# Output weights' last row tiles as units of seven products, semaphores awaited at their first users, and extra products at the layer seam

## The reference

```python
u = rmsnorm_2(h, pre_w)
proj = jnp.einsum('btd,de->bte', u, w_in)
...
pool_out = jax.nn.silu(pool_g) * pool_mixer(pool_v, pool_w, pool_scale)
ssd_out = ssd_mixer(ssd_xbc, ssd_z, ssd_dt, conv_w, conv_b, dt_bias, a_log, d_skip, ssd_norm_w)
attn = dsa_attention(q, k, v, qi, ki, i_w, topk).reshape(b, t, ATTN_WIDTH)
attn_out = jax.nn.silu(a_g) * attn
mix = jnp.concatenate([pool_out, ssd_out, attn_out], axis=-1)
out = jnp.einsum('bte,ed->btd', mix, w_out)
return h + rmsnorm_2(out, post_w)
```

## Time and profile before

| | us |
|---|---|
| median of three timed runs | 3298.12 |
| lowest, highest | 3296.45, 3301.9 |
| the profiled execution's own time | 3301.22 |
| its span, first to last instruction | 3299.4 |
| mean granted clock of PE, share of full | 0.994 |
| busy: PE, DVE, ACT, POOL | 3255.6, 1748.0, 770.1, 45.2 |

### The profile page before, as it was taken

One profiled execution on the slowest core, in us unless ns is written; L12 is line 12 of the kernel. 1 busy time (PEld: TensorE's weight loads), 2 busy tenths in 40 slices (PEclk: granted clock), 3 DMA queues, 4 the chain that ended last, 5 costly groups with the idle time before them and its releaser, 6 DMA issues.

```text
span 3299.4 us, 61922 instructions
## 1 busy us (share of the span) xinstructions
PE 3255.6 (99%) x26286; PEld 3003.9 (91%) x26286; DVE 1748.0 (53%) x3298; ACT 770.1 (23%) x2100; POOL 45.2 (1%) x83
## 2 busy tenths in 40 slices
PE   9999999999999999999999999999999999999999
PEld 7998899988999998988999997899879999988898
DVE  2545665414668651513455756666345566566652
ACT  1212322111111201211111226422131122353221
POOL 1000000000000000000000000000000000000000
PEclk9999999999999999999999999999999999999999
DMA  6453345453444304454444444433344545524432
GB/s 223 145 180 111 103 129 158 150 179 117 133 154 128 104 3 144 152 187 115 153 154 153 154 156 126 128 112 120 126 137 148 179 144 163 169 88 128 151 105 102
DMA packets 436210, 454.74 MB, mean 138 GB/s; under 512 B 25051, under 2 KB 412576, under 8 KB 435648
## 3 DMA queue, kind: packets, MB, share of 16 engines
q1 hardware_dynamic: 433344, 443.69, 42.5%
q0 software_dynamic: 2128, 5.19, 0.5%
q10 hardware_dynamic: 464, 1.90, 0.2%
HBM read 448.67 MB, written 2.10 MB: 137 GB/s over the span
## 4 chain that ended last, share of the span: by engine, by line
PE 95%; DVE 2%; ACT 1%; DVEq 1%; issue 0%; ACTq 0%; POOL 0%; POOLq 0%
PE bank L391 43%; PE bank L540 10%; PE bank L2340 9%; PE bank L319 5%; PE bank L2558 3%; PE bank L1965 3%; PE bank L1455 3%; PE bank L2450 1%; PE bank L2465 1%; PE bank L2486 1%; PE bank L2481 1%; PE bank L2475 1%; PE bank L2457 1%; PE bank L2469 1%; PE bank L2424 1%; PE bank L2544 1%
## 5 line engine op out<-in xcount | busy, mean ns | idle before, releaser
L391 PE MATMUL bank<-xnT,ring 128*128 128x128 f32 (+1 forms) x4800 | 593.0, 280 | 2.2 <-ACT wk L1115 1.0
L391 PEld LDWEIGHTS bank<-xnT,ring 128*128 128x128 f32 x4800 | 575.9, 191 | 5.7 <-issue 4.4
L540 PE MATMUL bank<-xnT,ring 128*128 128x256 f32 x1536 | 344.4, 383 | 0.4 <-ACT G L447 0.4
L391 PE MATMUL bank<-hT,ring 128*128 128x128 f32 (+1 forms) x2816 | 338.9, 279 | 0.6 <-ACT G L422 0.5
L391 PEld LDWEIGHTS bank<-hT,ring 128*128 128x128 f32 x2816 | 330.2, 191 | 1.2 <-ACT G L422 1.2
L540 PEld LDWEIGHTS bank<-xnT,ring 128*128 128x128 f32 x1536 | 290.6, 191 | 40.9 <-ACT G L447 0.6
L2340 PE MATMUL bank<-xnT,ring 128*128 128x272 f32 (+1 forms) x1344 | 310.9, 390 | 0.0
L2340 PEld LDWEIGHTS bank<-xnT,ring 128*128 128x128 f32 x1344 | 252.5, 190 | 44.5
L391 PE MATMUL bank<-G,ring 128*128 128x128 f32 (+1 forms) x2128 | 266.3, 278 | 0.0
L391 PEld LDWEIGHTS bank<-G,ring 128*128 128x128 f32 x2128 | 255.0, 191 | 0.2
L459 DVE TENSOR_TENSOR ring<-ring 128x1024 f32<-128x1024 f32 x100 | 122.5, 1225 | 236.6 <-PE bank L391 193.5
(11 more groups left out here) (632 smaller groups left out, 4304.8 us busy)
## 6 DMA issues: line engine op xcount, KB each, us to landing
ring<-in_w_in SPq DMA_DIRECT2D x155, 2048.0 KB, 8.3
ring<-in_w_out SPq DMA_DIRECT2D x16, 3072.0 KB, 11.8
ring<-in_w_out SPq DMA_DIRECT2D x16, 2048.0 KB, 10.6
ring<-in_w_br SPq DMA_DIRECT2D x12, 2048.0 KB, 8.3
ring<-in_w_in SPq DMA_DIRECT2D x6, 512.0 KB, 7.8
G<-in_x POOLq DMA_DIRECT2D x2, 1024.0 KB, 9.2
wk<-in_pool_w POOLq DMA_DIRECT2D x2, 1024.0 KB, 10.6
out<-G SPq DMA_DIRECT2D x8, 256.0 KB, 2.2
```

The lines of the kernel that those rows point to most:

```text
L391: mm = pe.matmul(out_, weights[:, k, :], x(k), start=(start and k == 0), stop=(k == half - 1), skip_group_check=True)
L540: mm = pe.matmul(bank[j][:, META:T], ring[:, s, k, j * P:(j + 1) * P], xnT[:, k, META:T], start=(k == 0), stop=(k == KT - 1))
```

## The change

The tail keeps its first two tiles plain and makes the other 14 by seven short units, as the merges do. Two tiles of each unit are added to `xnT` together, and the squares come in pairs; the first unit's turned inputs and sums are made under the plain tiles.

Several semaphores are awaited later, at the instruction that first needs them: the attention's end (`b2_pe`) at the eighth product of the tail, the merge's end (`merge_done`) at the thirteenth product of the block's end, `st_turned` inside the first unit, the zeroed part of `tok3` in ACT instead of PE. DVE scales inputs in the raw section when half of the second tile is done (`raw_half`), since that half has read the first eight. The gate and low-rank pieces go to bank 1, so that the next unit's bank 0 is free. The sums of the attention's fourth unit move ahead of the first head's scores in DVE's order, and ACT takes more copies ahead of the first head's exponentials. At the seam PE runs 12 products of a matrix of ones, whose result nobody reads.

```diff
@@ raw_section_pe / raw_tiles_dve
                     mm = pe.matmul(bank[j][:, 0:T], ring[:, s, k, j * P:(j + 1) * P], xnT[:, k, :],
                                    start=(k == 0), stop=(k == KT - 1))
+                    if t == 1 and k == KT // 2 - 1:
+                        mm.then_inc(S["raw_half"], 1)
...
-            v.wait_ge(proj_full, t0 + 2)
+            v.wait_ge(S["raw_half"], count["dve"]["raw_half"].go())
             for k in range(8):
                 normalise(k)
+            v.wait_ge(proj_full, t0 + 2)
             out(1).then_inc(proj_free, 1)
@@ mlstm_gates_pe, mlstm_act (rwkv_low_rank_pe, rwkv_act in the same way)
-            pe.wait_ge(proj_free, tiles["pe"].go(2) - 1)
+            pe.wait_ge(proj_free, tiles["pe"].go(2))
             for k in range(KT):
-                mm = pe.matmul(bank[0][0:36, 0:T], ring[:, 0, k, 0:36], xnT[:, k, :], start=(k == 0), stop=(k == KT - 1))
+                mm = pe.matmul(bank[1][0:36, 0:T], ring[:, 0, k, 0:36], xnT[:, k, :], start=(k == 0), stop=(k == KT - 1))
...
+            act.nop().then_inc(proj_free, 1)
             act.wait_ge(proj_full, tiles["act"].go(2))
...
-            act.activation(ROWS[:, FG, :], bank[0][32:36, 0:T], ACT.Copy).then_inc(proj_free, 2)
+            act.activation(ROWS[:, FG, :], bank[1][32:36, 0:T], ACT.Copy).then_inc(proj_free, 1)
@@ block_end_pe (and the wait ahead of its call)
+                    if t == k == 0:
+                        pe.wait_ge(S["part_used"], 3 * (BR - 1) - 1)
+                    if t == 0 and k == 12:
+                        pe.wait_ge(S["merge_done"], 3)
                     pe.matmul(bank[j][:, META:T], ring[:, s, k, j * P:(j + 1) * P], merged[:, k, META:T],
...
-            pe.wait_ge(S["merge_done"], 3)
@@ first units of a stretch (four places)
-                wait("st_turned")
-                    unit_pe(pe, unit_slot(u), unit_from(u, m0), x12, x22, x21, x11, unit_skip(u))
+                    unit_pe(pe, unit_slot(u), unit_from(u, m0), x12, x22, x21, x11, unit_skip(u),
+                            turned=None if u else count["pe"]["st_turned"].go())
@@ layers_pe, layer seam (SEAM = 12)
                     pe.wait_ge(proj_free, tiles["pe"].now(2))
+                    pe.wait_ge(work_free, work["pe"].now(1))
+                    for _ in range(SEAM):
+                        pe.matmul(wbank(work["pe"].now(1))[:, 0:P], ones, ones, start=True, stop=True)
                     raw_section_pe(pe, step)
@@ layers_pe, tail
-                wait("b2_pe")
                 pe.wait_ge(proj_free, tiles["pe"].now(2))
                 pe.wait_ge(S["so_act"], 6 * OUTS * (layer + 1))
-                for s in range(SLOTS):
-                    loaded(s)
-                    for j in range(4):
-                        ...
-                    if s == 2 and layer != LAST:
+                loaded(0)
+                for j in range(2):
+                    pe.wait_ge(proj_free, tiles["pe"].go())
+                    for k in range(W8):
+                        if j == 0 and k == W8 - 1:
+                            wait("b2_pe")
+                        mm = pe.matmul(bank[j][:, m0:T], wide[:, 0, k, j * P:(j + 1) * P], mix[SUB + k][:, m0:T],
+                                       start=(k == 0), stop=(k == W8 - 1))
+                    mm.then_inc(proj_full, 1)
+                for u in range(1, OUTS):
+                    unit_pe(pe, u // 2, m0, *tail_turned, skip=(1 if u == OUTS - 1 else 0), short=tail, part=u % 2,
+                            turned=count["pe"]["st_turned"].go() if u == 1 else None)
+                    if u == 5 and layer != LAST:
                         wait("p2_in", 16 * N_P2)
...
                 wait("rms_sq", KT)
+                pe.matmul(b[:, m0:T], ones, squares[:, KT - 2, m0:T], start=False, stop=False)
                 pe.matmul(b[:, m0:T], ones, squares[:, KT - 1, m0:T], start=False, stop=True).then_inc(work_full, 1)
@@ layers_load
-                tiles["sp"].go(16)
+                tiles["sp"].go(OUTS + 2)
@@ layers_act
+                        if half == 0 and i == 2:
+                            wait("tok_zero")
...
-                        out_copies(ahead + 7 + 5 * at)
+                        out_copies(ahead + (42 + 12 * min(at, 1) if h == 0 else 7 + 5 * at))
...
-                for k in range(KT):
+                def tail_squares(u):
                     wait("b2_in")
-                    act.activation(squares[:, k, m0:T], xnT[:, k, m0:T], ACT.Square, scale=SQ).then_inc(S["rms_sq"], 1)
+                    for k in (2 * u, 2 * u + 1):
+                        act.activation(squares[:, k, m0:T], xnT[:, k, m0:T], ACT.Square, scale=SQ).then_inc(S["rms_sq"], 1)
+                for u in range(1, OUTS):
+                    d1, d2 = (tail_parts[u % 2][:, j, :] for j in range(2))
+                    if u >= 3:
+                        act.wait_ge(S["tail_used"], (OUTS - 1) * layer + u - 2)
+                    unit_first_act(act, d1, m0)
+                    unit_second_act(act, d1)
+                    unit_third_act(act)
+                    unit_fourth_act(act, d2)
+                    tail_squares(u - 1)
+                    unit_last_act(act, d2, m0, 1 if u == OUTS - 1 else 0)
...
+                tail_squares(OUTS - 1)
                 rms_root_act(act, m0)
@@ layers_dve
+                    if u == 26:
+                        v.drain()
+                        for d in decay:
+                            v.memset(d[:, 416:L_END], 0.0)
+                        to("b2_pe")
...
-                v.memset(tok3[:, 2, :], 0.0)
-                for d in decay:
-                    v.memset(d[:, 416:L_END], 0.0)
-                v.drain()
-                v.nop().then_inc(S["b2_pe"], 1)
+                v.memset(tok3[:, 2, :], 0.0).then_inc(S["tok_zero"], 1)
...
+                out_sums12(4)
+                out_sum2(4)
                 wait("keep_ready", 3)
...
-                    if h == 0:
-                        out_sums12(4)
-                        out_sum2(4)
...
                 out_ends(OUTS - 1)
+                v.tensor_tensor(x12_, low[:, :, MID:T], low[:, :, META:MID], ALU.subtract)
+                v.tensor_tensor(x21_[:, :, META:MID], high[:, :, MID:T], low[:, :, MID:T], ALU.subtract)
+                if m0 == 0:
+                    v.tensor_scalar(x21_[:, :, 0:META], low[:, :, 0:META], -1.0, None, ALU.mult)
+                    v.tensor_copy(x11_[:, :, 0:META], high[:, :, 0:META])
+                v.drain()
+                v.tensor_tensor(x22_, high[:, :, MID:T], x12_, ALU.subtract)
+                v.drain()
+                v.tensor_tensor(x11_[:, :, META:MID], high[:, :, META:MID], x22_, ALU.subtract)
+                to("st_turned")
                 v.tensor_copy(gpost, vec2("post_norm_w_2", 16))
                 to("heads_done")
...
+                def tail_merge(u):
+                    v.drain()
+                    v.wait_ge(proj_free, tiles["dve"].now() + 2)
+                    pair = xnT[:, 2 * u:2 * u + 2, m0:T]
+                    v.tensor_tensor(pair, pair, tail_parts[u % 2][:, :, m0:T], ALU.add).then_inc(S["tail_used"], 1)
                     to("b2_in")
+                first_tile(0)
+                unit_sums12_dve(v, n0)
+                first_tile(1)
+                to("b2_in")
+                unit_sums34_dve(v, n0)
+                for u in range(1, OUTS):
+                    d1, d2 = (tail_parts[u % 2][:, j, :] for j in range(2))
+                    if u > 1:
+                        tail_merge(u - 1)
+                    unit_first_dve(v, d1, m0)
+                    if u + 1 < OUTS:
+                        unit_sums12_dve(v, n0 + u)
+                        unit_sums34_dve(v, n0 + u)
+                    if u > 1:
+                        tail_sums(u - 2)
+                    unit_ends_dve(v, d1, d2)
+                tail_sums(OUTS - 2)
                 v.nop().then_inc(S["rms_acc"], 1)
+                tail_merge(OUTS - 1)
```

More of the change, by code:

```diff
@@ L509, in build @@
         WARM = 8
+        SEAM = 12
         norm_uses = []
@@ L1406, in rwkv_low_rank_pe @@
             pe.wait_ge(w_loaded[0], 16 * uses["pe"][0].go())
[L1407 to L1408 removed]
+            pe.wait_ge(proj_free, tiles["pe"].go(2))
             for k in range(KT):
[L1410 removed]
+                mm = pe.matmul(bank[1][:, 0:T], ring[:, 0, k, 0:P], xnT[:, k, :], start=(k == 0), stop=(k == KT - 1))
             mm.then_inc(proj_full, 2)
@@ L3248, in layers_dve, with first_tile, tail_sums @@
                 out_ends(OUTS - 1)
+                tiles["dve"].go(OUTS)
+                x12_, x22_, x21_, x11_ = tail_turned
+                low, high = tail.first, tail.second
+                v.tensor_tensor(x12_, low[:, :, MID:T], low[:, :, META:MID], ALU.subtract)
[8 more added lines that the diff above has]
+                to("st_turned")
                 v.tensor_copy(gpost, vec2("post_norm_w_2", 16))
                 to("heads_done")
-                tiles["dve"].go(OUTS)
```

(14 more changed lines are left out.)

45 lines of the change are left out of this document (24 added, 21 removed).

## The result

The changed kernel takes 3272.6 us (median of four runs, 3269.1 to 3275.8), against 3298.6 us for the kernel before, measured beside it: a ratio of 0.992 (95% interval 0.9907 to 0.9932), 26.0 us less. In five further runs it took 3270.9 us, against 3297.7, a ratio of 0.9918 (0.9905 to 0.9932). Forecast were 3274.0 us, so 24.1 less than the median shown ahead. The profiled execution of the changed kernel took 3271.7 us, 29.5 less than that of before, where the sum of the terms was 25.9. The mean granted clock, 0.994 in the profiled execution of before, is 0.996 to 0.998 in all four runs.

A forecast was written before the change was run, and what follows sets the result against it. The prediction took TensorE's stream of products to bound the kernel. Terms of 10.4 - 2.0 + 9.5 + 3.0 + 5.0 = 25.9 took 3301.2 to 3275.3 us, then 3274 with a third of 3.1 carried over; range 3267 to 3286.

The forecast's parts named there:

- The tail: Each layer's last 16 tiles: units cut them to 53.6 and 50.7 us, gaining 10.4, less 2.0 at the ends.
- the slower rival: Tail's small products: weight loads pace them, up to +89 us, kernel slower; chance 0.03.
- the estimate of +39 us: Tail's 784 short passes: by the skill's ratio each costs 0.05 us more for its load, a slower kernel.
- The estimate of 5.3 us of work: Tail units: DVE's sums and additions take 5.3 us each, against 6.25 to 6.6 of PE.
- The 6.4 with drains: Tail units: DVE needs some 6.4 us each once drains are included.
- the rival of a pacing DVE: Tail: DVE needs 6.4 to 6.9 us a unit, 3 to 7 us given back, 3277 to 3281; chance 0.14.
- The end of the chain: Tail's last product to the root's Ln: copy, pair and second square add 1.0 a layer, 2.4 becoming 3.4 us.
- Waits: PE waits at several places, moved to the first user: 1.1 + 1.9 + 1.6 + 3.4 + 1.5 = 9.5 us gained.
- The rival of returning waits: PE's next semaphores: freed waits come back there, only the tail's gain is left, 3290 us; chance 0.10.
- Unit 4's sums: Attention: 5.3 us of PE waits go, 1.0 and 1.3 come at the probabilities' transposes, net 3.0 gained.
- The clock: Slow stretches at block's end, unit 4 and seam go: 1.7 + 1.6 + 1.7, 5.0 us gained.
- a third of the median's 3.1: Whole time: a third of the 3.1 us between profiled execution and timed median is carried over, giving 3274 us.

The follow-up runs named there:

- The two kernels that isolate it: Changed kernel with its tail as 16 plain tiles again, ratio 0.9948; kernel before with only the tail made units, ratio 0.9978.
- one more addition of 1.22: Changed kernel with one more DVE addition of 1024 elements, read by nobody, in six of the tail's seven units; ratio 0.9930 to the kernel before.
- the tail alone: Kernel before with only the tail as units, every wait where it stood and no extra products; ratio 0.9978 to the kernel before.
- the sums back: Changed kernel with unit 4's sums behind the first head's scores again and ACT's copies as before; ratio 0.9938 to the kernel before.
- the zeroing back: Changed kernel with the zeroing of tok3 and two small pieces ahead of PE's transposes again; ratio 0.9943 to the kernel before.

## Why the prediction was right

**The tail.** 53.8 and 50.7 us against 53.6 and 50.7: the durations taken from the merges' passes and from the large units carry over. The two kernels that isolate it give 7.2 and 7.3 for tail and end together, where the sum had 8.4. The plain tail takes 58.9 and 55.3 us there, not the 59.2 and 55.5 of the earlier trace rows, which is half of the difference; the rest was not traced.

**Loads of weights.** PE's units are without holes at the pace of the merges and the loads' total is the same 3003.9 us, so the slower rival, and with it the estimate of +39 us from the ratio of the Trainium skill (TensorE: Matmul & The Clock Gate, Back-to-back issue gap), is refuted for these passes.

**DVE.** The estimate of 5.3 us of work stands (4.7 to 4.8 busy, some 5.4 at its own pace). The 6.4 with drains, which made the rival of a pacing DVE worth 0.14, was too high by 1.0: with it, one more addition of 1.22 would have made a step of 7.6 us, and it takes 6.65 to 6.73.

**The end of the chain.** 3.45 for 3.4, and copy, pair and second square do join it. The prediction does not name the longest link, the table load of 1.28 us ahead of Ln. It was in the 2.4 of before already, beside PE's passes, which ended 0.1 later there, so the sum holds without it.

**Waits.** Those forecast to go are gone, and put back they return at their old lengths, with at most 0.2 taken up by the next wait (zeroing; from the kernel before to the changed one that wait grew by 0.4). The rival of returning waits, 3290, is what the tail alone gives (0.9978, 3291).

**Unit 4's sums.** The net of 3.0 was 2.4: 5.33 of waits went, 2.94 came. Against the changed kernel with the sums back, where the second wait is 3.17 and not 2.81, it is 2.8. The new waits are 1.37 and 1.02 where 1.0 and 1.3 were worked out, and 0.55 for the second sum in layer 1, which the walk through layer 0 could not show.

**The clock** is the term that was mis-sized: 5.0 were taken back. The kernel before spent 1.3 more in layer 1 behind the wait at L2386 (0.9 beyond the waits for ACT's copies that stand there now), which the prediction did not look for; the seam alone is worth 2.8, not 1.7; and unit 4's waits can cost 1.7 and 2.7. Against that, the block's end does not lose its 1.7 in every execution. Of the 3.6 us by which the profiled execution fell more than the sum, 3.0 lie in the first stretch, where the same code differs by as much, 0.7 in layer 1 and 0.4 at the seam. That only a part of such stretches is in every run was the reason to carry over a third of the median's 3.1; the medians fell by 26.0 and 26.9, the forecast by 24.1. That the sum of 25.9 came so near to the medians is in part luck: the tail with its end gave 1.1 to 1.2 less than its term and unit 4's sums 0.6 less, and the clock's surplus (1.1 at the seam, 1.3 in layer 1) happens to make up for them.

## What to carry to other kernels

Cut the span at steps that all versions share and compare stretch by stretch: here four of six repeat within 0.02 us between two executions, and within 0.4 among all kernels that share the code, so that 1 us can be told in one profile where the time itself scatters by 5. A wait of the engine that bounds the kernel is worth its length and what its clock loses behind it, so price both, and look for slow stretches behind every wait, not only the long ones; one of those here stands behind no wait at all. An engine that runs close to the pace of another may slip unseen in the middle; look at the first thing that needs all of its work, since the slip is paid there.

## What the runs showed of the hardware

**Waits and the clock.** At the four places of the change (seam, block's end, unit 4's sums, transposes before the SSD stage) 18 waits of PE of 1.7 to 4.0 us stand in the 14 profiled executions. Behind 12 of them the granted clock is 0.50 for a stretch: 3 of 3 at the seam (4.0 us), 2 of 3 at the block's end (2.0), 4 of 6 at unit 4 (2.5 to 3.2), 3 of 6 at the transposes (1.7). In the 66 cases where these waits were removed or cut short (1.66 us at most), it is 1.00 each time. Length alone does not decide: 3.07 left it at full in the kernel with the tail alone, 1.7 brought it down in the one with the zeroing back. A wait is not needed either: in 13 of the 14 executions the clock is 0.50 for a stretch with or right behind the 32 passes of 16 columns (L1996 of the changed kernel, 3.64 us) at the block's end, with no wait of PE before it, and it costs 1.7 us where it lasts 3.4.

**VectorE beside GpSimd.** In both layers the first moved sum (L3162) took 2.01 us while POOL's select ran, the second, behind it, 1.76, which is also what the first takes where no select lies beside it. The Trainium skill (SBUF — State Buffer, SBUF: two separate sides) says that VectorE and GpSimd share one pair of ports, held exclusively for a whole instruction, also by a VectorE operation with two SBUF inputs against a GpSimd one that reads SBUF. The trace agrees in direction: the select of 0.41 us began 0.02 before the sum. A block up to its end would be 0.39 us, and the sum lost 0.25; the trace's spans on GpSimd are rough, and no run here separates the two.
